# Sample blocks' output-gate and merge-gate projections and the backward chunks moved among block 0's experts

## What is computed

```python
h = rms_norm(x, g_mix_pre) * (1 + sc_a) + sh_a
z, xbc, dt, q, k, v, o, gate, merge = split(h @ w_in)
y  = ssd_scan(xbc, forward) + flip(ssd_scan(xbc, backward)) + skip
y  = rms_norm(y * silu(z)) @ w_ssd_out
hm = mlstm_scan(q, k, v, forward) + flip(mlstm_scan(q, k, v, backward))
hm = (rms_norm(hm) * sigmoid(o)) @ w_mlstm_out
g_ssd, g_ml = split(sigmoid(merge))
x1 = x + gt_a * rms_norm((g_ssd * y + g_ml * hm) @ w_out)
h2 = rms_norm(x1) * (1 + sc_f) + sh_f
for each token and each of 8 heads:
    16 experts chosen by two top-16 searches; gate = softmax(scores)
    f += sum(gate * gelu(u_tab[e] . h2) * v_tab[e])
out = x1 + gt_f * rms_norm(f)
```

## Time and profile before

| what | value |
|---|---|
| profiled execution, its time | 2931.15 us |
| its span, first to last instruction | 2929.4 us |
| median of 3 runs | 2928.61 us |
| busy: PE, VectorE, ScalarE, GpSimd | 86%, 52%, 31%, 27% of the span |
| moved | 937.87 MB, 320 GB/s over the span |
| stages: before the units, units, merge 0 | to 330 us, to 828 us, to 935 us |
| first window, later windows | 356 us, about 400 us each |

### The profile page before, as it was taken

One profiled execution on the slowest core, in us unless ns is written; L12 is line 12 of the kernel. 1 busy time (PEld: TensorE's weight loads), 2 busy tenths in 40 slices (PEclk: granted clock), 3 DMA queues, 4 the chain that ended last, 5 costly groups with the idle time before them and its releaser, 6 DMA issues.

```text
span 2929.4 us, 26241 instructions
## 1 busy us (share of the span) xinstructions
PE 2532.2 (86%) x8274; PEld 1316.1 (45%) x8274; DVE 1530.9 (52%) x3684; ACT 906.3 (31%) x2427; POOL 803.6 (27%) x705
## 2 busy tenths in 40 slices
PE   6999999889857889989889899898899898877876
PEld 3555554344324644445444355444455443433332
DVE  2320031111012875669755678755698557666674
ACT  3100110000012342354423364423445334333332
POOL 0111100000000333333333333333433334444453
PEclk8999999999988999999999999999999999999999
DMA  5222234542355899999999999999999999999996
GB/s 215 94 94 94 108 137 169 191 155 99 145 201 191 335 421 420 421 420 371 397 421 421 410 406 377 421 420 415 420 402 387 420 421 421 407 421 417 420 414 286
DMA packets 138173, 937.87 MB, mean 320 GB/s; under 512 B 16514, under 2 KB 20866, under 8 KB 35378
## 3 DMA queue, kind: packets, MB, share of 16 engines
q0 software_dynamic: 98720, 694.73, 57.7%
q1 hardware_dynamic: 33698, 200.58, 18.0%
q10 hardware_dynamic: 5616, 40.90, 3.5%
HBM read 898.33 MB, written 37.81 MB: 320 GB/s over the span
## 4 chain that ended last, share of the span: by engine, by line
DMA 31%; PE 22%; DVE 9%; ACT 3%; DVEq 2%; issue 2%; POOL 1%; ACTq 0%; SPq 0%; POOLq 0%
DMA e_expert<-in_peer_uv,e_idx 30%; PE e_acc L1604 14%; DVE e_expert L1722 4%; PE e_qs L1619 2%; PE e_B L1537 1%; POOL e_expert L1401 1%; ACT e_diag L1490 1%; DVEq L1724 1%; PE e_A L1537 1%; DMA e_wb<-in_w_out 1%; ACT e_coef L1485 1%; ACT e_act L1482 0%; ACTq L1486 0%; PE e_A L905 0%; PE e_acc L1596 0%
## 5 line engine op out<-in xcount | busy, mean ns | idle before, releaser
L1604 PE MATMUL e_acc<-e_expert,e_diag 128*128 128x512 f32 x2560 | 1215.8, 623 | 246.0 <-ACT e_diag L1490 245.7
L1401 POOL DMA_INDIRECT e_expert<-in_peer_uv,e_idx x640 | 761.2, 1189 | 1311.0 <-PE e_acc L1604 1120.6
L1722 DVE CUSTOM_DVE_ANT_0 e_expert<-e_expert,e_xb 128x1024 f32<-128x1024 f32 x640 | 777.1, 1224 | 516.6 <-DMA e_expert<-in_peer_uv,e_idx 496.5
L1604 PEld LDWEIGHTS e_acc<-e_expert,e_diag 128*128 128x128 f32 x2560 | 489.7, 199 | 885.6 <-issue 525.5
L547 PE MATMUL pj<-w_chunk,hT 128*128 128x512 f32 x800 | 364.0, 613 | 30.0 <-DMA w_chunk<-in_w_big 27.9
L1482 ACT ACTIVATE e_act<-e_dots 128x2 f32<-128x2 f32 x320 | 65.1, 203 | 883.9 <-DVEq L1724 875.7
L547 PEld LDWEIGHTS pj<-w_chunk,hT 128*128 128x128 f32 x800 | 155.7, 197 | 221.8 <-issue 219.0
L1490 ACT ACTIVATE e_diag<-ident,e_coef 128x128 f32<-128x128 f32 x640 | 221.9, 394 | 22.9 <-issue 1.1
L513 PE MATMUL pj<-hT,w_chunk 128*128 128x512 f32 x512 | 225.2, 593 | 0.0
L1485 ACT ACTIVATE e_coef<-e_act,e_gate 128x1 f32<-128x1 f32 x640 | 153.7, 287 | 23.5 <-issue 1.7
L1619 PEld LDWEIGHTS e_qs<-e_h2T,e_w_head 128*128 128x128 f32 x1280 | 148.2, 192 | 9.8 <-issue 9.6
(11 more groups left out here) (377 smaller groups left out, 2026.7 us busy)
## 6 DMA issues: line engine op xcount, KB each, us to landing
e_wb<-in_w_out SPq DMA_DIRECT2D x60, 1024.0 KB
e_w_head<-in_w_q ACTq DMA_DIRECT2D x39, 1024.0 KB
w_chunk<-in_w_big SPq DMA_DIRECT2D x18, 2048.0 KB, 9.1
w_chunk<-in_w_mod SPq DMA_DIRECT2D x8, 2048.0 KB, 8.9
scratch_proj<-tile_out POOLq DMA_DIRECT2D x10, 1280.0 KB
e_expert<-in_peer_uv,e_idx POOLq DMA_INDIRECT x640
wm<-in_w_mod SPq DMA_DIRECT2D x4, 2048.0 KB, 18.2
e_m<-scratch_mod_rows SPq DMA_DIRECT2D x15, 512.0 KB, 7.9
```

What stands on the lines that cost most here:

```text
L1401: nc.gpsimd.indirect_dma_start(expert[:, u % RING, :], None, dr["peer_uv"], bass.IndirectOffsetOnAxis(idx[:, h % 4, s:s + 1], 0)).then_inc ...
L1604: mm = nc.tensor.matmul(acc[:, c * 512:(c + 1) * 512], diag[:, (u + j) % RING, :], expert[:, (u + j) % RING, D + c * 512:D + (c + 1) * 512 ...
L1722: nc.vector.tensor_tensor_reduce(expert[:, u % RING, 0:D], expert[:, u % RING, 0:D], xb[p % 2][:, :], 1.0, 0.0, ALU.mult, ALU.add, dots[:, ...
```

## The change

The units of the chunks 4 to 9 (o and the merge gates) are done for block 0 only in the projection stage. For blocks 1 to 4 they are done in the first window of the experts, as 24 late units: a late unit is two blocks by 256 columns. Their weights are loaded once more, in 12 loads of 1 MB, into buffers of the merge; ACT copies each result and issues its store. The three back chunks go there too, 48 steps over the groups 4 to 31, with their own loads of x, keys and v. In the second half of the first window, from group 32 on, scan and merge of block 1 run at two steps a group, after the late units and back chunks are through; x and qk of block 1 are loaded there and no longer ahead. Of block 0's experts, those of the heads 0 to 2 and every second one of the heads 3 to 5 are multiplied and summed by VectorE, one group behind their dot products, without diagonal and PE product; VectorE adds `acc` at the end of the block. `hT` stays in SBUF and shares its place with later tiles. The projection stage gets a third weight buffer and weaves one scan step to a unit.

```diff
+W_BUFFERS = 3
+LATE_FROM = 4
+LATE = [2 * c + half for c in range(LATE_FROM, COLS_T // 512) for half in range(2)]
+LATE_UNITS = 2 * len(LATE)
...
-        chunks = [("prompt", 0)] + [("back", b) for b in range(CHUNKS, 1, -1)]
+        chunks = [("prompt", 0)]
...
-            units += [(at, kind, c, b) for b in range(BLOCKS if kind == "big" else 1)]
+            units += [(at, kind, c, b) for b in range(BLOCKS if kind == "big" and c < LATE_FROM else 1)]
...
-        scan_list = [(0, s) for s in range(FULL_STEPS)] + [(j, s) for j in range(1, len(chunks)) for s in BACK_STEPS]
+        scan_list = [(0, s) for s in range(FULL_STEPS)]
...
-                    for j, s in scan_list[done:done + 2]:
+                    for j, s in scan_list[done:done + 1]:
                         scan(j, s)
-                    done += 2
+                    done += 1
...
+                last = n - W_BUFFERS
+                if last < X_CH:
+                    sp.wait_ge(x_mm, 4 * (last + 1))
+                elif last < X_CH + Q_CH:
+                    sp.wait_ge(q_mm, 4 * (last - X_CH + 1))
+                else:
+                    sp.wait_ge(unit_mm, end_of[last - X_CH - Q_CH])
+                j = n % W_BUFFERS
...
+        elif s == 2 and back_keys is not None and j + 1 < N:
+            sp.wait_ge(B_turned, j + 1)
+            load_x(j + 1)
+        elif s == 17 and back_keys is not None and j + 1 < N:
+            sp.wait_ge(K_turned, j + 1)
+            load_qk(j + 1)
...
+ON_VECTOR = [u < 3 * TOPK or u < 6 * TOPK and u % 2 == 0 for u in range(HEADS * TOPK)]
+FIRST_ON_PE = 3
+BACK_LIST = [(j, s) for j in range(CHUNKS - 1) for s in BACK_STEPS]
...
+        def window_one(at):
+
+            units = [at // 2 - 1] if at < 16 and at >= 2 and at % 2 == 0 else [at - 8] if 15 <= at < LATE_UNITS + 8 else []
+            backs = range(max(0, len(BACK_LIST) * (at - 4) // 28), max(0, min(len(BACK_LIST), len(BACK_LIST) * (at - 3) // 28)))
+            steps = range(2 * (at - 32), 2 * (at - 32) + 2) if at >= 32 else range(0)
+            return units, [BACK_LIST[i] for i in backs], steps
...
+                    if p == 1:
+                        units, backs, steps = window_one(at)
+                        for u in units:
+                            late(u)
+                        for j, s in backs:
+                            back(j, s)
+                        for step in steps:
+                            at_step(1, step)
...
+            def first_region_free():
+                sp.wait_ge(backs_done, CHUNKS - 1)
+                sp.wait_ge(late_mm, LATE_UNITS)
+                for j in range(2):
+                    sp.wait_ge(late_out[j], 16 * LATE_UNITS // 2)
+                sp_back_end()
+                load_x(0)
+                load_qk(0)
...
+            def late_load(i):
+                sp.dma_start(late_w[i % 2], dr["w_late"][i]).then_inc(late_in[i % 2], 16)
...
+                elif u % 2 == 0 and i + 1 < len(LATE):
+                    sp.wait_ge(late_mm, u)
+                    late_load(i + 1)
...
-                elif x == 50 and p + 1 < BLOCKS:
+                elif x == 50 and p and p + 1 < BLOCKS:
...
-                    pool.wait_ge(slot_free, u - RING + 1)
+                    pool.wait_ge(vector_free if ON_VECTOR[u - RING] else slot_free, earlier(u - RING) + 1)
...
+            def late_result(u):
+                i, pair = LATE[u // 2], u % 2
+                if u >= 2:
+                    act.wait_ge(late_out[u % 2], 16 * (u // 2))
+                act.wait_ge(late_mm, u + 1)
+                nc.scalar.copy(late_from[u % 2], late_to[u % 2])
+                act.drain()
+                act.sem_inc(late_free, 1)
+                act.dma_start(dr["proj"].rearrange("b p n -> p b n")[:, 1 + 2 * pair:3 + 2 * pair, 256 * i:256 * (i + 1)],
+                              late_from[u % 2].rearrange("p (b n) -> p b n", n=256)).then_inc(late_out[u % 2], 16)
...
+            def late(u):
+                i, pair = u // 2, u % 2
+                if pair == 0:
+                    pe.wait_ge(late_in[i % 2], 16 * (i // 2) + 16)
+                if u >= 2:
+                    pe.wait_ge(late_free, u - 1)
+                for b in range(2):
+                    tokens = slice((1 + 2 * pair + b) * P, (2 + 2 * pair + b) * P)
+                    for k in range(KT):
+                        last = nc.tensor.matmul(late_to[u % 2][:, 256 * b:256 * (b + 1)], hT[:, k, tokens], late_w[i % 2][:, k, :],
+                                                start=(k == 0), stop=(k == KT - 1))
+                last.then_inc(late_mm, 1)
...
+            def vector_products(m, n):
+                u = m * TOPK + 2 * n
+                mine = [v for v in (u, u + 1) if ON_VECTOR[v]]
+                if mine:
+                    dve.wait_ge(diag_ready, m * GROUPS + n + 1)
+                for v in mine:
+                    by = coef[:, n % 4, v - u:v - u + 1]
+                    value = expert[:, v % RING, D:2 * D]
+                    if v == 0:
+                        nc.vector.tensor_scalar(f[:, :], value, by, None, ALU.mult).then_inc(vector_free, 1)
+                    else:
+                        nc.vector.scalar_tensor_tensor(f[:, :], value, by, f[:, :], ALU.mult, ALU.add).then_inc(vector_free, 1)
+                    dve.drain()
...
                     dot_pair(m, n)
+                if m * GROUPS + n > 0:
+                    vector_products(m - (n == 0), (n - 1) % GROUPS)
+                if m == HP and n == 0:
+                    first_sum()
```

More of the change, by code:

```diff
@@ L457, in store_row @@
                 sp.dma_start(dr["mod_rows"][:, i * 512:(i + 1) * 512], mpar[:, 0, :]).then_inc(row_out, 16)
-            for n in range(2, X_CH + Q_CH + 1):
+            for n in range(W_BUFFERS, X_CH + Q_CH + W_BUFFERS):
                 load(n)
-            load(X_CH + Q_CH + 1)
             def scan(j, s):
@@ L594, in token_result @@
                     return
-                n = token_at[k] // BLOCKS
+                n = sum(unit[1] == "big" and unit[3] == 0 for unit in units[:k + 1]) - 1
                 if b == 0:
@@ L714, in scan_steps @@
     half = (B[:, 0:512], B[:, 512:1024])
-    own = lambda name: sem("s_" + name)
+    own = lambda name: sem(tag + name)
+    own_full = own if any(kind != "back" for kind in kinds) else (lambda name: None)
+    own_sample = own if "sample" in kinds else (lambda name: None)
+    back_keys = w.get("back_keys")
+    keys_of = lambda k: qkT[:, KT + k, :] if back_keys is None else back_keys[:, k, :]
     x_in, qk_in, v_in, H_in, C_in, m_in = own("x_in"), own("qk_in"), own("v_in"), own("H_in"), own("C_in"), own("m_in")
@@ L1004, in dve_step @@
                 nc.vector.memset(v[:, :, DM:CE], 1.0)
-            if kind == "back" and kinds[j - 1] == "prompt":
-                dve.wait_ge(out, 16 * 7)
+            if kind == "back" and j == 0:
                 nc.vector.tensor_copy(mp[:, 1, :], t["rows"][:, R_M0 + HM:R_M0 + 2 * HM])
@@ L1205, with earlier, experts @@
 PIECE_AT = (34, 35, 37, 39, 41, 42, 44, 46, 48, 49, 51, 53)
+ON_VECTOR = [u < 3 * TOPK or u < 6 * TOPK and u % 2 == 0 for u in range(HEADS * TOPK)]
+FIRST_ON_PE = 3
+BACK_LIST = [(j, s) for j in range(CHUNKS - 1) for s in BACK_STEPS]
 PIECES = ((0, 0, 0), (0, 0, 1), (1, 0, 0), (1, 0, 1), (0, 1, 0), (0, 1, 1), (1, 1, 0), (1, 1, 1), (2, 0, 0), (2, 1, 0), (2, 0, 1), (2, 1, 1))
-def experts(nc, dr, t):
+def earlier(u):
+    return sum(ON_VECTOR[v] == ON_VECTOR[u] for v in range(u))
+def experts(nc, dr, t, hT):
     with ExitStack() as ctx:
@@ L1390, in _ @@
             sp.dma_start(keys[:, :, :], dr["keysT"]).then_inc(keys_in, 16)
-            interleave(scan, merge, prepare, body, finish)
+            interleave(late, back, scan, merge, prepare, body, finish)
         @block.gpsimd
@@ L1645, in inverse, with first_region_free, back, late @@
                 nc.vector.tensor_scalar(mss[:, col:col + n], mss[:, col:col + n], scale, eps, ALU.mult, ALU.add)
+            def first_region_free():
+                dve.wait_ge(late_mm, LATE_UNITS)
+                for j in range(2):
+                    dve.wait_ge(late_out[j], 16 * LATE_UNITS // 2)
             def scan(j, s):
-                dve_scan(j, s, lambda: dve.wait_ge(piece_mm, 12 * (j + 1)))
+                dve_scan(j, s, (lambda: dve.wait_ge(piece_mm, 12 * (j + 1))) if j else first_region_free)
+            def back(j, s):
+                dve_back(j, s, (lambda: dve.wait_ge(piece_mm, 12)) if j == 0 else None)
+            def late(u):
+                pass
             def merge(p, x):
@@ L1828, in _ @@
             dve_scan_init()
+            dve_back_init()
             nc.vector.memset(zero[:, :], 0.0).then_inc(const_ready, 1)
-            interleave(scan, merge, prepare, body, finish, body_first=True)
+            interleave(late, back, scan, merge, prepare, body, finish, body_first=True)
 def programme(nc, dr):
@@ L1888, in layout @@
     out["w_big"] = tiles(cat(z, v, o, m, xbc, q, k))
```

(1 more changed line is left out.)

183 lines of the change are left out of this document (116 added, 67 removed).

## The result

The changed kernel takes 2849.59 us (median of 4 runs, 2847.9 to 2851.46) where the kernel before, on the same chip, takes 2928.91: ratio 0.9728, 95% interval 0.9711 to 0.9745. It is 79 us faster; forecast were 46 (2883, range 2825 to 2942).

What follows compares the result with a forecast made beforehand. PE was taken to bound the projection stage and transfers the expert stage. 2931.15 us profiled, minus 218 in the projection stage, plus 172 in the first expert window, gave 2885, or 2883 at the runs' median; range 2825 to 2942.

Steps and rivals of the forecast that it cites:

- The projection stage loses 218 us: Stage from 330 us: 232 us of PE work and waits removed, 11 and 3 against; ends 205 and 232.
- The pairs: Projection stage's last six unit-and-modulation-chunk pairs: 16 us each for two queued 2 MB loads, against 14.2 of PE; costs 11.
- The third buffer, 28 + 12 = 40: Projection stage: PE's waits for w_chunk end, 27.9 us, and slow first units after six waits go, 12 more.
- Merge 0 no change: Merge 0, 828 to 935 us: keeps its instructions and its 107 us, no extra waits.
- Groups 1 to 32, 82 + 150 = 232: First window's first half: 82 us by PE plus exchange, then 150 with PE, VectorE and DMA ending within 3 us.
- The stop: At group 33: PE, ScalarE, then VectorE wait behind step 0 for block 1's x and qk loads, 20 us.
- Groups 33 to 64 behind the stop, 276: First window's second half: scan stretch 138 us by VectorE, then merge stretch 138 us by DMA.
- Nothing later changes: Blocks 1 to 4 after the first window: instructions kept, no change in time.
- A: Rival, first window: engines overlap so each stretch costs its bare limit; growth 109 us, time 2820; chance 0.23.
- B: Rival, first window: PE, ScalarE and VectorE work adds in series within groups; 96 us more, time 2979; chance 0.12.
- C: Rival, projection stage: the last six unit-and-modulation-chunk pairs take 20 us each, 24 more, time 2907; chance 0.11 without the clock.
- C's clock: Rival, projection stage: the six pairs run wholly at PE's lower clock, 54 us more, time 2937; chance 0.04.

Runs made afterwards that it cites:

- six-head run: The changed kernel with all experts of block 0's heads 0 to 5 on VectorE, 24 more products: 2863.36 us, ratio 0.9774.
- early loads alone: The changed kernel with block 1's x and qk loaded earlier at group 33, VectorE's store wait later, and back chunks' v at step 2: 2826.0 us, ratio 0.964.
- two heads on VectorE: The changed kernel with x, qk and v loaded earlier and only block 0's heads 0 and 1 on VectorE: 2820.85 us, repeated 2817.51.

## Why the prediction was right, and where its sizes were off

Right in direction, in mechanism and in most places; the time lay 33 us under it, inside the range and at the lower edge of the forecast's own 2850 to 2915. The largest misses are the projection stage, 22 us too small, and groups 17 to 32, 25 too large; groups 1 to 16 and the second half, 9 each the other way, hide part of them, so the closeness of the sum is in part luck. Its first reading of the earlier trace rows is off too: PE is at eight or nine tenths in slices 2 to 11, not at nine in 2 to 15, and DMA at nine from slice 15. Its sum doesn't use that. By its steps:

- **The projection stage loses 218 us: 240.** Three terms were off.
  - The pairs, "I take 16": with three buffers they run at PE's pace, 13.5 to 14.8 us but for the first, which holds the one long gap (17.7), not at the loads'. The 16 comes nearer the kernel with two buffers (17 to 19 measured). I priced two queued loads of 2 MB close to the rate of one after the other; three deep, the stage moved 335 GB/s in 502 to 587 and DMA had a share of 0.88. The 11 us against the change, and the 3 for the prompt's states, were not there.
  - A wait that I hadn't counted: the back chunks' own inputs held PE up in the kernel before, by its waits in 330 to 828:

```profile
PE pj L821 <- DMA s_turned<-scratch_xbcT: 16.0, 2, 12.4
...
PE pj L942 <- DMA s_v<-scratch_proj: 1.4, 1, 1.4
```

  - These 17.4 us left with them. My 26 for the back chunks was PE's work alone.
  - The third buffer, 28 + 12 = 40: alone it gave 29.5. The waits went; of the slow units the row tells 8.8 us (busy of the units' line, 364.0 in the earlier trace rows, 355.2 in that run), and the wait for v grew from 1.4 to 6.3. 232 + 17 - 10 = 239. That 17 not foreseen and 10 too many partly cancel is luck.
- **Merge 0 no change:** +2, right. The first head stood at 696.5 (said 717) and the window ended at 1216.1 (said 1245), 520 us long (said 528).
- **Groups 1 to 32, 82 + 150 = 232: 91 + 125 = 216.** The sum of PE's parts, 79 + 134 = 213, is what was measured; the 16 us on top because "Three engines end within 3 us of each other" were not, nor the 3 for the exchange. PE was busy 206 of 216 us, and the run with an eighth of the late products shows the others some 40 us behind it. VectorE was less busy than said: 100 us in groups 17 to 32, not 123, as 28 dots and 28 products fell there, not 32 of each. That the first half is 9 over and the second 25 under is in part the cut: ten late units (322 of 768 instructions) lie ahead of the third query copy, not nine.
- **The stop, 20 us with its wait on the load from the scratch: 19.3**, with the row that was named for it; taken away it gives 14.7. The wait for v (6.9) was not foreseen; it gives 8.4 by the medians.
- **Groups 33 to 64 behind the stop, 276: 284.** VectorE 0.85 in the scan stretch (0.9 said) and 0.70 in the merge stretch with DMA at 0.98, as the two-part sum has it. The products of heads 4 and 5 are free there and those of head 3 are not, which the six-head run shows.
- **Nothing later changes:** -6 us. The window of block 1 took 402 us after and 409 before, and in the twelve runs, which leave these blocks' instructions alone, between 401 and 410. I assign these 6 us to nothing.

**The rivals.** A (better overlap, 2820, a window under 480): half right. Groups 1 to 32 did run at the bare limit, but the stop was there and scan and merge did not share; the window was 520. With the stop removed by hand the time is 2826, near A's, but not by A's way: the window is 495.5, still over 480. B (groups in series) fell: the window was far from 574, and PE was 0.93 busy in groups 17 to 32. C (the pairs wait) fell with the third buffer: the six pairs took 84 us, not over 115. With two buffers it is half true: 26 us of waits.

C's clock: of the six units behind a wait with two buffers four took 8.68 to 9.11 us and two 7.10 and 7.11, and the length of the wait doesn't sort them (8.69 after 3.04, 7.10 after 3.43); with three buffers the one after 6.46 us took 9.53, and the granted clock over the six pairs was 0.96. So the pair wholly at the lower level did not occur. The Trainium skill (TensorE: Matmul & The Clock Gate, HAM oscillation — how this bites in real kernels) tells of a loop whose compute is shorter than its wait for DMA. A pair here is 13.5 us of PE behind a wait of 2.8 to 6.6 us, so the prediction's 2937 "by that rule" took the rule outside its condition, and no run here tests it.

**Not tested.** No run puts the late units back, or gives all of block 0's products back to PE. That the units' PE time left the stage is read from their line: count 800 to 416, busy 364.0 to 186.6 us.

## What to carry to other kernels

When work is moved out of a stage, count what waits with it: its own loads held PE 17 us in the old stage beside 26 us of its work, and when such work was left behind after the units had gone it cost 69. Where one engine is the limit and others come close, sum that engine; here an allowance of 19 us for exchanges, with no wait in a trace behind it, was not needed. At a switch between phases list the loads of the next phase and ask what each must wait for: moving x and qk ahead of the wait for stores gave 15 us, and v at an earlier step with them 24, nearly as much as a third buffer of 2 MB.

## What the runs showed of the hardware

- The same small store lands in 2 or in 15 us. The 24 late stores (256 KB each) took 2.1 to 15.2 us, median 9.6: 2.12 to 2.18 in three cases where the DMA share during the store was 0.36 or 0.37, 15.16 at a share of 1.00, and the last one, which the stop waits for, 11.65 at 1.01. The Trainium skill (DMA: Bandwidth & Descriptors, Queues, rings and completion order) says that each DMA engine takes turns between the queues with work, a packet at a time; the trace agrees with it but doesn't show the turns.
- PE's granted clock was lower where another engine led: 0.63 in the stop, where PE stood still, 0.74 in the scan stretch that VectorE limits, 1.00 in groups 1 to 16. With the early loads alone (0.70 from the switch on) the scan's products took 1.45 to 1.54 times as long as with two heads on VectorE (0.87). So giving PE's work to VectorE can go with slower work on what is left on PE.
- Two accumulating products in a row took 2.66 to 2.67 us on VectorE; 2 x 1.37 was assumed.
